# A hybrid convolution and attention layer in fp32: another queue for the centred rows, a fourth place for weight factors, another order of the last units

## The reference, cut to what matters

```python
z = jnp.einsum("bsd,de->bse", h, w_in) + b_in
glu_val, glu_gate, gate_c, q, k, v, f_logit, gate_a = _split_columns(z)
y_conv = _conformer_conv(glu_val, glu_gate, w_dw, b_dw, g_cn, b_cn)   # taps, then layer norm, SiLU
y_conv = y_conv * jax.nn.silu(gate_c)
y_attn = _forgetting_attention(q, k, v, f_logit)   # logits + cum[q] - cum[k], cum = cumsum(log_sigmoid(f))
y_attn = y_attn * jax.nn.silu(gate_a)
y = jnp.concatenate([y_conv, y_attn], axis=-1)
sub = jnp.einsum("bse,ed->bsd", y, w_out) + b_out
h = _layer_norm(DN_ALPHA * h + sub, g_post, b_post)
```

## Time and profile before

| | us |
|---|---|
| time, median of 3 runs | 1633.11 (1632.91 to 1633.67) |
| the profiled execution, its own time | 1634.14 |
| its span | 1632.4 |
| PE busy in it | 1566.7 (96%) |
| PEld busy | 1492.5 (91%) |
| DVE busy | 1442.6 (88%) |
| ACT busy | 838.4 (51%) |
| POOL busy | 274.8 (17%) |

### The profile page before, as it was taken

How to read it: one execution, slowest core, us unless ns; L and a number is a source line. 1 busy time by engine, 2 the same in 40 slices (tenths; PEclk the granted TensorE clock), 3 DMA queues, 4 the chain that set the end, 5 groups by cost and what they waited for, 6 DMA issues and landing times.

```text
span 1632.4 us, 29443 instructions
## 1 busy us (share of the span) xinstructions
PE 1566.7 (96%) x11574; PEld 1492.5 (91%) x11574; DVE 1442.6 (88%) x1952; ACT 838.4 (51%) x1224; POOL 274.8 (17%) x295
## 2 busy tenths in 40 slices
PE   7999999999999999999999999999977999999995
PEld 7999999999999999999999999998977877778884
DVE  7669999999999999999999999999865679886885
ACT  4465454554554545545455455454443566644461
POOL 1011212122122121221212212201222100010000
PEclk9999999999999999999999999999989999999998
DMA  8488988999999999999999999998988998687673
GB/s 224 102 193 190 223 206 202 241 225 234 222 215 231 233 223 235 207 249 225 210 233 237 226 216 220 243 227 190 245 207 207 317 321 321 205 282 220 230 230 137
DMA packets 316761, 367.33 MB, mean 225 GB/s; under 512 B 14593, under 2 KB 254369, under 8 KB 315313
## 3 DMA queue, kind: packets, MB, share of 16 engines
q1 hardware_dynamic: 287184, 264.65, 52.7%
q0 software_dynamic: 27360, 100.68, 34.1%
q10 hardware_dynamic: 2080, 0.13, 0.1%
HBM read 286.73 MB, written 87.06 MB: 229 GB/s over the span
## 4 chain that ended last, share of the span: by engine, by line
PE 70%; DVE 13%; DMA 7%; issue 6%; ACT 3%; POOL 0%; SPq 0%; DVEq 0%; ACTq 0%; POOLq 0%
PE ps L1043 23%; PE ps L1044 23%; PE ps L1045 23%; DVE whl L1284 3%; DMA conv_rows_dram<-cin 2%; DVE c_tiles L1385 2%; DVE whl L1287 2%; ACT whl L748 1%; PE ps L1156 1%; DMA raw<-raw 1%; DVE yl L1537 1%; DMA raw<-out_sums_dram 1%; DMA raw<-in_w_in_dram 1%; ACT aff_c L992 1%; DVE yc L1598 1%
## 5 line engine op out<-in xcount | busy, mean ns | idle before, releaser
L1043 PE MATMUL ps<-xh,whl 128*128 128x256 f32 x3136 | 897.1, 286 | 35.5 <-ACT nu L845 23.5
L1044 PE MATMUL ps<-xl,whl 128*128 128x256 f32 x3136 | 889.7, 284 | 0.0
L1045 PE MATMUL ps<-xh,whl 128*128 128x256 f32 x3136 | 889.7, 284 | 0.0
L772 ACT ACTIVATE whl<-raw 128x1024 fp32r<-128x1024 f32 x392 | 415.3, 1061 | 594.1 <-PE ps L1045 467.5
L1043 PEld LDWEIGHTS ps<-xh,whl 128*128 128x128 f32 x3136 | 601.9, 192 | 39.8 <-ACT nu L845 24.1
L1044 PEld LDWEIGHTS ps<-xl,whl 128*128 128x128 f32 x3136 | 602.3, 192 | 0.3 <-issue 0.2
L1045 PEld LDWEIGHTS ps<-xh,whl 128*128 128x128 f32 x3136 | 601.9, 192 | 0.0
L1284 DVE TENSOR_TENSOR whl<-raw,whl 128x1024 fp32r<-128x1024 f32 x392 | 481.8, 1229 | 83.8 <-ACT whl L772 83.5
L1385 DVE SCALAR_TENSOR_TENSOR c_tiles<-ps,taps,c_tiles 128x511 f32<-128x511 f32 (+14 forms) x480 | 350.0, 729 | 6.9
L1287 DVE TENSOR_TENSOR whl<-raw,whl 128x1024 fp32r<-128x1024 f32 x106 | 129.5, 1221 | 57.7 <-ACT whl L748 57.7
L1043 PE MATMUL ps<-whl,yh 128*128 128x512 f32 x424 | 167.9, 396 | 10.4 <-DVE yl L1537 7.3
(11 more groups left out here) (177 smaller groups left out, 1313.7 us busy)
## 6 DMA issues: line engine op xcount, KB each, us to landing
raw<-in_w_in_dram SPq DMA_DIRECT2D x224, 512.0 KB, 7.8
raw<-raw POOLq DMA_DIRECT2D x112, 512.0 KB, 5.8
out_sums_dram<-in_w_out_dram POOLq DMA_DIRECT2D x64, 512.0 KB, 9.5
raw<-out_sums_dram SPq DMA_DIRECT2D x64, 512.0 KB, 5.0
raw<-in_w_out_dram SPq DMA_DIRECT2D x48, 512.0 KB, 4.7
out_sums_dram<-in_w_out_dram SPq DMA_DIRECT2D x32, 512.0 KB, 9.5
out_sums_dram<-out_sums_dram SPq DMA_DIRECT2D x32, 512.0 KB, 9.6
x<-in_x_dram SPq DMA_DIRECT2D x8, 512.0 KB, 8.1
```

Source lines behind the costliest of these rows:

```text
L772: nc.scalar.activation(w_high(n), source(n), ACT.Copy).then_inc(high_done, 1)
L1043: nc.tensor.matmul(o, ah, bh, start=start, stop=False, skip_group_check=True)
L1044: nc.tensor.matmul(o, ah, bl, start=False, stop=False, skip_group_check=True)
L1045: return nc.tensor.matmul(o, al, bh, start=False, stop=True, skip_group_check=True)
```

## The change

Five things are changed. (1) The centred rows are stored by ACT's queue, ahead of the square of the same row; SP has only the loads of `cin` left there. (2) The weight factors of the output projection have a fourth place, `whl_more`, from unit 5 (`FOUR`) on, and are made three units ahead (`AHEAD`). (3) `finish_conv` and `gated` stand one u later after `norm`, `NORM_AT` ends two u earlier, and the results of product 7 are taken at u = 42 to 45 instead of 44 to 47. (4) `END` is 6, all six with places of their own; the two tiles of n = 0 go unit by unit (both tiles of a unit, then the next unit), the tiles of n = 1 one after the other as before. (5) In group 0 PE does the last forget terms ahead of the last turns of x, the last bank of x turned is `R5`, which was no bank of x before, the wait for all of x stands at product 4 of group 0 and product 5 of group 1, and ACT's and DVE's `forget` stand earlier.

```diff
-NORM_AT = (4, 6, 8, 10, 12, 14, 17, 20, 23, 26, 29, 32, 34, 36, 38, 40)
-END = 8
+NORM_AT = (4, 6, 8, 10, 12, 14, 16, 19, 22, 24, 27, 30, 32, 34, 36, 38)
+END = 6
+FOUR = 5
+AHEAD = 3
...
+            return R5 if j == X_BANKS - 1 else (BANK_A, BANK_B, BANK_C, R1_ODD)[j % 4]
...
         def out_w(u, low):
+            if u >= E0:
+                return w_end[u - E0][:, low, :]
+            if u < FOUR:
                 return whl[:, out_n(u) % SLOTS, low, :]
+            slot = (3, 1, 2, 0)[(u - FOUR) % 4]
+            return whl_more[:, low, :] if slot == 3 else whl[:, slot, low, :]
...
-            def store_cent(j):
-                sp.wait_ge(cent_done, j + 1)
-                sp.dma_start(conv_dram[j, :, :], cin[:, j % 4, :]).then_inc(cent_stored[j % 4], 16)
             def load_cin(j):
                 if j >= 4:
-                    store_cent(j - 4)
                     sp.wait_ge(sq_done, j - 3)
                     sp.wait_ge(cent_stored[j % 4], 16 * (j // 4))
...
-            for j in range(HEADS - 4, HEADS):
-                store_cent(j)
...
+                if u < FOUR:
                     act.wait_ge(unit_done, out_n(u) - 2)
...
+                elif u < E0:
+                    act.wait_ge(unit_done, out_n(u) - 3)
...
             def square(j):
                 act.wait_ge(cent_done, j + 1)
                 if j >= 2:
                     act.wait_ge(sq_added, j - 1)
+                nc.scalar.dma_start(conv_dram[j, :, :], cin[:, j % 4, :]).then_inc(cent_stored[j % 4], 16)
                 nc.scalar.activation(c_tiles[:, j % 2, :], cin[:, j % 4, :], ACT.Square).then_inc(sq_done, 1)
...
             for u in range(1, E0):
-                high(out_n(u + 2))
+                if u <= 2:
+                    high(out_n(u + 2))
+                if u >= 2:
+                    high(out_n(u + AHEAD))
...
-                    if u == NORM_AT[j] + 1:
+                    if u == NORM_AT[j] + 2:
                         finish_conv(j)
...
-                if g == 1 and m == 1:
+                if g == 1 and m in (1, 5):
+                    pe.wait_ge(xl_done, X_BANKS if m == 5 else X_BANKS - 4)
+                if (g, m) == (0, 4):
                     pe.wait_ge(xl_done, X_BANKS)
...
                     if g == 0 and s == 5:
+                        f_terms(((3, 5, 1),)).then_inc(f_done, 1)
+                        for b in range(3):
+                            turn_x(2, b)
                         pe.wait_ge(dw_loaded, 16)
...
                         last.then_inc(rows_turned, 1)
-                        f_terms(((3, 5, 1),)).then_inc(f_done, 1)
+                        turn_x(2, 3)
...
-            for n in range(2):
+            for u in range(E0, OUT_UNITS):
+                ready(u)
                 for g in range(2):
-                    for u in range(E0, OUT_UNITS):
-                        if n == 0 and g == 0:
-                            ready(u)
-                        last = out_mm(u, n, g)
-                    last.then_inc(end_done, 1)
+                    last = out_mm(u, 0, g)
+                    if u == OUT_UNITS - 1:
+                        last.then_inc(end_done, 1)
+            for g in range(2):
+                for u in range(E0, OUT_UNITS):
+                    last = out_mm(u, 1, g)
+                last.then_inc(end_done, 1)
...
-                    if u == NORM_AT[j] + 2:
+                    if u == NORM_AT[j] + 3:
                         gated(j)
```

More of the change, by code:

```diff
@@ L207, in build @@
         over.close()
+        sb("parts_b", [P, 2048], F32, over)
+        whl_more = sb("whl_more", [P, 2, 1024], F32R, over)
+        over.close()
         sb("parts_a", [P, 2 * PT_LEN], F32, over)
@@ L220, in build @@
         yl = sb("yl", [P, 2, SEQ], F32R, over)
-        yh_end = sb("yh_end", [P, 2, SEQ], F32R, over)
-        yl_end = sb("yl_end", [P, 2, SEQ], F32R, over)
         over.close()
@@ L233, in build @@
         nu1 = sb("nu1", [P, TOK])
+        yh_end = sb("yh_end", [P, SEQ], F32R, over)
+        yl_end = sb("yl_end", [P, SEQ], F32R, over)
+        over.close()
         c_tiles = sb("c_tiles", [P, 2, SEQ])
@@ L322, in y_pair @@
         def y_pair(ring_y, end, v):
-            last = v - E0 // 2
-            return end[:, last, :] if 0 <= last < 2 else ring_y[:, v % 2, :]
+            return end[:, :] if v == E0 // 2 else ring_y[:, v % 2, :]
         def out_bank(m, n, g):
@@ L938, in _ @@
                         x_high(4)
-                    if (g, s) in ((0, 6), (1, 1)):
-                        forget(g)
+                    if (g, s) == (0, 6):
+                        forget(0)
                     evict(g, s)
@@ L952, in _ @@
                         x_high(2)
+                        forget(1)
                     if g == HEAD_GROUPS + 2 and s == 6:
@@ L1031, in _ @@
                     scale_rows(2 if u == 93 else 3)
-            for u in range(E0 + 2, OUT_UNITS):
-                high(out_n(u))
-                if u % 2 == 0:
-                    y_high(u // 2)
+            for v in range(E0 // 2 + 1, OUT_PAIRS):
+                y_high(v)
+                if E0 + AHEAD <= 2 * v:
+                    high(out_n(2 * v))
+                high(out_n(2 * v + 1))
             deviation(2)
@@ L1101, in turn_x @@
                     pe.wait_ge(xl_done, j - 3)
+                if x_bank(j) == R5:
+                    pe.wait_ge(c12_done, 1)
                 for kk in range(2):
@@ L1190, in _ @@
                         f_terms(((1, 1, 0),))
-                    if g == 0 and s in (3, 4, 5):
+                    if g == 0 and s in (3, 4):
                         for b in range(4):
-                            turn_x((6, 5, 2)[s - 3], b)
+                            turn_x((6, 5)[s - 3], b)
                     if g == 0 and s == 3:
@@ L1556, in _ @@
                         sum_1(g + 1)
-                    if g == 1 and s in (0, 2):
-                        forget(s)
+                    if (g, s) == (1, 1):
+                        forget(1)
                     evict(g, s)
@@ L1637, in results @@
                     first_product(1, n, g, n, 0, ALU.add)
-                if u in (44, 45, 46, 47):
-                    n, g = divmod(u - 44, 2)
+                if u in (42, 43, 44, 45):
+                    n, g = divmod(u - 42, 2)
                     product_done(7)
@@ L1725, in _ @@
             for u in range(1, E0):
-                low(out_n(u + 2))
+                if u <= 2:
+                    low(out_n(u + 2))
+                if u >= 2:
+                    low(out_n(u + AHEAD))
                 if u % 2 == 0:
@@ L1741, in _ @@
                 early_rows(u)
-            for u in range(E0 + 2, OUT_UNITS):
-                low(out_n(u))
-                if u % 2 == 0:
-                    y_low(u // 2)
+            for v in range(E0 // 2 + 1, OUT_PAIRS):
+                y_low(v)
+                if E0 + AHEAD <= 2 * v:
+                    low(out_n(2 * v))
+                low(out_n(2 * v + 1))
             dve.wait_ge(bout_added, 32 * NT)
```

24 lines of the change are left out of this document (8 added, 16 removed).

## The result

The changed kernel takes 1613.57 us (median of 4 runs, 1612.13 to 1617.09) against 1633.39 for the kernel before beside it: ratio 0.9879, 95% interval 0.9859 to 0.9899. It is faster by 19.8 us. I had forecast 45, and a range of 1580 to 1606: the direction was right, the size was not, and the time lies outside the range.

A forecast was written before the change was run, and what follows sets the result against it. PE was taken as the bound, busy 1566.7 of 1632.4 us, so only its stalls and lower clock could be regained. Gains 24 + 6 + 7.5 + 8.2 = 45.7 off 1634.1, less 1.0, gave 1588 us; range 1580 to 1606.

The forecast's parts named there:

- Centre: Groups 52 to 54: storing centred rows through ACT's queue frees SP's loads, gain 24 us, bounds 14 to 28.
- I leave 4 us of the 28.0 lost: Groups 52 to 54: of 28.0 us lost (88.6 against 60.6), 4 stay, so the gain is 24.
- the DMA engines bind the centre: Groups 52 to 54: 74.6 us of busy DMA time is the floor, only 14 gained, about 1600; chance 0.18.
- Output projection: Output projection: ACT no longer waits for norm with factors behind it, gain 7.5 us, bounds 3 to 9.5.
- they get about 6.5 us to land, where the median is 5.5: Output projection: weights queued behind SP's gate load, which waits for `gated`, still land in time, with 1 us margin.
- a mild rival at 0.08: Output projection: landings of 7.5 us stall PE 1 us at each of 12 gate loads, 1607; chance 0.08.
- The slower rival: Output projection, u = 8 to 38: late gate loads cost 12 x 4 = 48 us, 1643; chance 0.04.
- only issue time is saved: Centre: SP saves only 6 us of issue time and loads stay late, about 1605; chance 0.05.
- The start: Groups 1 and 2: an earlier forget chain removes the wait for `tiles`, gain 6 us, bounds 3 to 8.
- The fourth place: Output projection: a fourth place for factors, said to cost nothing by itself; no separate gain given.
- The end: Last units: the new order starts the last add at about 1612.9 instead of 1621.09, gain 8.2 us, bounds 4 to 8.5.

The follow-up runs named there:

- e3: The changed kernel with the centred rows stored by SP ahead of the loads again: 1630.59 us, ratio 0.9963 to the kernel before.
- e4: The kernel before with only the centred rows' stores moved to ACT's queue: 1619.74 us, ratio 0.9898.
- e2: The changed kernel with most bytes of the centred-row stores and, from group 51, of POOL's weight-sum DMAs left out: 1603.46 us, ratio 0.9806.
- e1: The changed kernel with SP's gate load behind the weights of unit NORM_AT[j - 4] + 11 instead of + 8: 1601.87 us, ratio 0.9794.
- e9: The kernel of e1 with part 3 undone and the gate load at + 10, four places kept: 1610.01 us, ratio 0.9833.
- e7: The kernel of e1 with three factor places, two units ahead, and the gate load at + 10: 1602.96 us, ratio 0.9795.
- e5: The kernel before with part 4 alone (END 6, n = 0 unit by unit), three places kept: 1628.01 us, ratio 0.995.
- e11: The kernel of e1 with three late weight sums moved into the output projection and POOL's product 7 sum before the last square addition: 1598.09 us, ratio 0.9778.

## Why the prediction missed, step by step

- **Centre, 24 forecast, 12.8 measured net.** The mechanism was right, and so was its place: SP's waits for landed stores fell from 43.4 us to 15.7, the first weights went out at +9.0, and e3 and e4 give the part 14 to 17 us. The term that was mis-sized is "I leave 4 us of the 28.0 lost". 11.2 of them stayed, and 4.3 more were given back behind. I had reckoned with `B11` alone. It came in time; `B21` did not, whose place in `raw` came free later and which then took 13.3 us in group 52. I had taken the landing of the weights as it was in the kernel before, where they went out into traffic that SP itself had stretched (208 to 231 GB/s; 254 to 273 now), and e2 shows that with fewer bytes the whole residue goes. I had the share of 0.99 in group 51 before me and read it as harmless. It was not quite: in the changed kernel group 51 ran unstalled at 1.00, but its `B21` landed 11.9 us after it had its place, and PE stood 0.88 us for it one unit into group 52.
- **The rival "the DMA engines bind the centre"** had the right resource and a wrong floor: 74.6 us of busy share are no bound, since the three groups took 71.8. Its gain of 14 in the centre was nearer to the 12.8 than my 24 was; that its price fitted is luck, since it was worked out from that floor. What stalls PE is when a block lands, not how many busy us there are.
- **Output projection, 7.5 gained forecast, 4.5 lost measured.** This is the largest miss, 12 of the 25.9 us between forecast and trace. The failed step is "they get about 6.5 us to land, where the median is 5.5". I called it the thinnest thing in the change and priced it as a mild rival at 0.08. The 6.5 us took SP's issue as given. But the issue waits for `gated`, which stands on DVE behind a low factor, and this waits for ACT's high factor and so for weights that SP issued late for the same reason. The median landing in the stretch 1290 to 1450 was 6.2 for weights, with single ones at 8 to 15, and ACT's waits for them were up to 3.6 us. The factors three ahead put the gate load one step earlier in time and `gated` moved one step back, so SP was held for three steps instead of one. e1 shows that this alone was worth 13.9 us; e9 shows that part 3 is worth 6.4 of the 7.5 that I had hoped for, as soon as SP is free. The wait for norm that I had blamed did go, as forecast.
- **The slower rival** (SP held by the gate loads) was the right place. It was far from its price of 4 us at each of 12 places: the miss is 12 us in all, and half of what the output projection lost against e1 lies at one place, output units 16 to 19.
- **The rival "only issue time is saved"** gave 6 us for the centre; e4 measured 16.7. The Trainium skill ("DMA: Bandwidth & Descriptors", section "Issuing engines are not separate DMA queues") says that all issuers share the same engines and that their transfers interleave. With that half the trace agrees: SP's weights landed in 10.0 instead of 6.7 us, waits for a place not counted, once ACT's stores ran beside them. With the other half, that several issuers save sequencer time alone, this case does not agree, since SP's queue also waited in order for the stores to land (43.4 us), and e4 gave 16.7 us where issue time was 6.
- **The start, 6 forecast.** 4.6 in the middle of group 2, 4.3 at the centre. The wait for `tiles` shrank from 3.5 only to 2.1; I had set it to nothing in the sum and named as the lower bound, 3, that PE comes earlier too.
- **The fourth place, nothing forecast.** Right (e7), although in e7's expectation I gave it 4 to 8 us, which was wrong.
- **The end, 8.2 forecast, 7.2 measured**, 8.2 by e5 alone, and the last two adds 8.64 us apart where I had said 8 to 9.

The terms of the range were added as if each could fail only on its own. The centre and the output projection failed together, and each by more than the residue that I had left it.

## What to carry to other kernels

When a wait in a queue's program order is taken away, price what then follows at the landing times of denser traffic, not at those of the stalled kernel: the stall had thinned it. Do this for every block that the next step needs, not only for the first one issued. Before a queue's waiting instruction is moved against the rest, write down the loop through it (who issues, what lands, who computes, who releases the queue) and count the steps that it holds the loads behind it; here one number in SP's order was worth 14 us. Here a place more in a ring gave nothing once the gate loads were in time (e7).

## What the runs showed of the hardware

The DMA share of the profile did not tell stalled groups from unstalled ones: group 51 ran without a stall at 0.99 before and 1.00 after, and the stalled groups had 0.82 to 0.87 before the change and 0.95 to 0.96 after it. The median time from issue to landing of the same 512 KB load did not either: it was 6.8 us in the kernel before, which had the longest stalls, and 13.3 in the changed kernel; at 9.1 (e2) groups 52 to 54 had no stall, and at 9.3 (e11) PE still waited 1.4 and 2.8 us for low factors. A stall needs both numbers, when the block could go out and how long it then took. And the time from issue to landing takes in waiting when SP's issuing instruction waits for a place: of the 15.5 us of `B21` in group 52, 2.3 were that. The 13 issues on ACT's queue between 1182 and 1255 took 0.33 us each, where I had allowed up to 1.3, and PE's wait for `nu`, the copy that follows them most closely, is 0.2 us in all.
